# A hybrid encoder step on one core: ScalarE makes the third factor of the queries' norms behind its copy of the values and the keys' squares instead of ahead of them

## What is computed

```python
def mla_queries(cq_raw, pos, q_a_norm, w_q_up, q_nope_norm, q_rope_norm):
    B, T, _ = cq_raw.shape
    q = (rmsnorm(cq_raw, q_a_norm) @ w_q_up).reshape(B, T, MLA_HEADS, QK_NOPE + QK_ROPE)
    q_nope = rmsnorm(q[..., :QK_NOPE], q_nope_norm)
    q_pe = rope(rmsnorm(q[..., QK_NOPE:], q_rope_norm), pos)
    return q_nope, q_pe

def mla_expand(ckv, w_kv_up, k_nope_norm):
    B, S, _ = ckv.shape
    kv = (ckv @ w_kv_up).reshape(B, S, MLA_HEADS, QK_NOPE + V_HEAD)
    return rmsnorm(kv[..., :QK_NOPE], k_nope_norm), kv[..., QK_NOPE:]
```

## Time and profile before

| | before |
|---|---|
| median of 3 runs | 1995.39 us (1994.79 to 1996.48) |
| the profiled execution | 1995.78 us |
| its span, first to last instruction | 1994.0 us |
| PE busy | 1985.5 us (100%) |
| DVE busy | 1254.3 us (63%) |
| ACT busy | 911.5 us (46%) |
| POOL busy | 192.7 us (10%) |
| granted TensorE clock, mean | 0.999 |

### The profile page before, as it was taken

The page is one execution under the profiler, slowest core; times in us unless marked ns, Lnnn a source line. Parts: engine busy times, 40 slices in busy tenths (PEclk is TensorE's granted clock), DMA queues, the critical chain, the costliest instruction groups (busy, mean ns, idle before and its releaser), DMA issues.

```text
span 1994.0 us, 36219 instructions
## 1 busy us (share of the span) xinstructions
PE 1985.5 (100%) x14762; PEld 1961.7 (98%) x14762; DVE 1254.3 (63%) x2474; ACT 911.5 (46%) x1810; POOL 192.7 (10%) x228
## 2 busy tenths in 40 slices
PE   9999999999999999999999999999999999999998
PEld 9999999999999999999999999999999999999998
DVE  7856677677576786868777555444455664444444
ACT  5564456565444443434444444444444553333333
POOL 0011143433200000000000001000000000000000
PEclk9999999999999999999999999999999999999999
DMA  9765443333455554645545655565556556666665
GB/s 249 197 187 157 113 120 117 99 111 119 122 170 147 149 169 128 179 127 175 157 145 170 169 169 168 168 170 168 173 169 171 169 183 193 193 193 193 193 193 142
DMA packets 219262, 323.24 MB, mean 162 GB/s; under 512 B 28240, under 2 KB 100264, under 8 KB 219096
## 3 DMA queue, kind: packets, MB, share of 16 engines
q1 hardware_dynamic: 215800, 317.71, 55.3%
q10 hardware_dynamic: 3296, 3.22, 0.5%
HBM read 310.06 MB, written 9.62 MB: 160 GB/s over the span
## 4 chain that ended last, share of the span: by engine, by line
PE 99%; DVE 0%; DMA 0%; ACTq 0%; ACT 0%; issue 0%
PE bank L1884 31%; PE bank L1887 30%; PE bank L1888 30%; PE bank L2150 1%; PE bank L2120 1%; PE bank L2046 1%; PE bank L2049 1%; PE bank L2048 1%; PE bank L2222 0%; PE bank L2248 0%; PE bank L2116 0%; PE bank L2117 0%; DMA xt<-in_meta_tokens_dram 0%; PE bank L2260 0%; PE bank L2064 0%; PE bank L2065 0%
## 5 line engine op out<-in xcount | busy, mean ns | idle before, releaser
L1215 DVE TENSOR_TENSOR wlo<-raw,whi 128x512 fp32r<-128x512 f32 (+1 forms) x1256 | 811.0, 655 | 681.5 <-ACT whi L801 671.5
L1884 PE MATMUL bank<-xsplit,whi 128*128 128x288 f32 (+2 forms) x4128 | 1217.2, 295 | 2.4 <-DVE xsplit L1239 2.1
L1888 PE MATMUL bank<-xsplit,wlo 128*128 128x288 f32 (+2 forms) x4128 | 1212.1, 294 | 0.0
L1887 PE MATMUL bank<-xsplit,whi 128*128 128x288 f32 (+2 forms) x4128 | 1211.9, 294 | 0.0
L801 ACT CAST whi<-raw 128x512 fp32r<-128x512 f32 (+1 forms) x1256 | 706.8, 576 | 954.9 <-PE bank L1888 911.6
L1884 PEld LDWEIGHTS bank<-xsplit,whi 128*128 128x128 f32 (+1 forms) x4128 | 773.2, 187 | 5.1 <-issue 3.4
L1887 PEld LDWEIGHTS bank<-xsplit,whi 128*128 128x128 f32 (+1 forms) x4128 | 773.2, 187 | 2.0 <-issue 1.0
L1888 PEld LDWEIGHTS bank<-xsplit,wlo 128*128 128x128 f32 (+1 forms) x4128 | 772.8, 187 | 0.0
L1884 PE MATMUL bank<-latents,whi 128*128 128x288 f32 (+1 forms) x352 | 112.7, 320 | 0.2
L1887 PE MATMUL bank<-latents,whi 128*128 128x288 f32 (+1 forms) x352 | 106.9, 304 | 0.0
L1888 PE MATMUL bank<-latents,wlo 128*128 128x288 f32 (+1 forms) x352 | 106.7, 303 | 0.0
(11 more groups left out here) (301 smaller groups left out, 1254.8 us busy)
## 6 DMA issues: line engine op xcount, KB each, us to landing
raw<-in_w_in_dram SPq DMA_DIRECT2D x313, 512.0 KB, 3.8
raw<-in_w_out_dram SPq DMA_DIRECT2D x128, 512.0 KB, 3.8
raw<-in_w_in_dram SPq DMA_DIRECT2D x142, 256.0 KB, 3.1
raw<-in_w_q_up_dram SPq DMA_DIRECT2D x48, 384.0 KB, 3.3
raw<-in_w_kv_up_dram SPq DMA_DIRECT2D x16, 512.0 KB, 3.7
xres<-in_x_prompt_dram SPq DMA_DIRECT2D x32, 128.0 KB, 3.7
xt<-in_x_prompt_dram SPq DMA_DIRECT2D x28, 128.0 KB, 4.9
out_dram<-ytok SPq DMA_DIRECT2D x28, 128.0 KB, 3.5
```

The source lines that it names most:

```text
L1215: ins = tt(lo, src, hi.bitcast(f32), ALU.subtract)
L1884: ins = mm(out, w_hi, m_hi, start=start, stop=False, **kw)
L1887: mm(out, w_hi, m_lo, start=False, stop=False, **kw)
L1888: return mm(out, w_lo, m_hi, start=False, stop=stop, **kw)
```

## The change

`q_rstd` takes a list of the factors to make. Behind unit 15 (unit 14 in the first pair) it now makes the first two; the third is made at the end of `pair_end`, behind the copy of the values and the two squares of the keys.

```diff
-            def q_rstd(phase, i, n):
+            def q_rstd(phase, i, n, tiles):
 
-                for t in range(3):
+                for t in tiles:
                     b = 4 + t
...
                 k_square_hi(phase, i, n, 0)
                 k_square_hi(phase, i, n, 1)
+                q_rstd(phase, i, n, (2,))
...
                 if k == 14:
-                    q_rstd("bulk0", 0, 0)
+                    q_rstd("bulk0", 0, 0, (0, 1))
...
                     if k == 15 and phase == "step":
-                        q_rstd(phase, i, j + 1)
+                        q_rstd(phase, i, j + 1, (0, 1))
```

## The result

The changed kernel takes 2000.82 us, median of 10 runs (1999.94 to 2001.42), beside 1995.47 us for the kernel before in runs on the same chip: 1.0025 times as long, 95% interval 1.0017 to 1.0033. It is slower by some 5 us, where 4.7 were forecast. Its profiled execution has a span of 1999.0 us, 5.0 more than before.

A forecast was written before the change was run, and what follows sets the result against it. TensorE bounds, meeting the ACT-DVE-POOL chain without slack. 6 x 0.79 x 0.96 = 4.55 plus 0.3 for the first pair, 4.85, taken as 4.7, gave 2000.5 profiled, 2000.1 us predicted; range 1996.4 to 2001.6.

The forecast's parts named there:

- PE and the chain meet with no slack: At the transposes PE waits for POOL's probabilities, so 0.96 of a delay in the chain reaches the pair's end.
- The copy of the values is not held by the factor: At a pair's end the copy waits for PE's last matmul, starting 0.04 us behind it.
- a little faster: Rival: the copy of the values starts sooner and PE's 0.16 us stall shrinks; at most 1.1 us, 1994.3; chance 0.03.
- Casts 0.87 later, unit 3 0.32 later, turn 1.9 later: Delays in us at a pair's end: ACT's casts, unit 3 reaching DVE, and POOL's turn of the queries.
- Lost turns: DVE held by POOL running beside it: 0.28 us by the turn, 0.88 by four copies, against 0.69 before.
- Both close encounters: POOL's second copy against DVE's unit 4 first part, DVE not held; third copy against first scaling, POOL first.
- one turn fewer: Rival: DVE's first scaling precedes POOL's third copy, so a turn of 0.22 to 0.26 us falls away; 1998.7; chance 0.20.
- The rule of the Trainium skill: Shared SBUF ports go to whichever of DVE and POOL starts first; taken literally, chain about 0.87 us later, 2000.7.
- Scalings end 0.79 later: DVE's scaling of queries, and the chain behind it, moves 0.32 + 0.28 + 0.88 - 0.69 us in six pairs.
- Not slower: POOL out of DVE's way: Rival: today's three lost DVE turns (0.69 us) vanish and cover the casts' delay; 1995.4; chance 0.17.
- The sum: Six pairs give 4.55 us, the first 0.3: 4.85, taken as 4.7 since pair 398's late exponentials may cover some.
- The last pair: At 500 us the next group's maxima wait 1.12 us for PE, not this chain, so cost 0.

The follow-up runs named there:

- short copies in the kernel before: Kernel before with POOL's four copies of turned queries 72 instead of 288 columns wide, the rest left out: 1995.13 us, ratio 0.9998.
- the last experiment: Changed kernel, Ln and Exp moved behind units 3 and 4's casts, and PE's third tile of unit 0 behind unit 1's first two: 1994.01 us, ratio 0.9992.
- late casts alone: Kernel before with four idle ACT copies ahead of the casts of units 3 to 5 in seven pairs: 1995.87 us, ratio 1.0001.
- a late turn alone: Kernel before with POOL's turn of the queries waiting for ACT's cast of unit 4 of the next pair: 1996.07 us, ratio 1.0003.
- both put in by hand: Kernel before with four idle ACT copies ahead of the casts and POOL's turn waiting for the last of them: 2000.69 us, ratio 1.0026.

## Why the prediction was right

Predicted 2000.1 us, measured 2000.8, and by the path that was forecast.

- *Bounds: PE and the chain meet with no slack.* Shown from both sides: 0.73 earlier gains nothing (short copies in the kernel before), 0.37 later at the exponentials costs 0.35 a pair.
- *The copy of the values is not held by the factor.* It starts 0.04 behind PE's last matmul in both kernels, now with 0.94 idle ahead. The rival "a little faster" fell with it. That its price was well estimated shows in the last experiment: the stall of 0.16 a pair is real, but to win it the tile has to move, not the factor.
- *Casts 0.87 later, unit 3 0.32 later, turn 1.9 later.* Measured 0.87, 0.32 (2.89 against 2.57) and 1.91 (2.54 against 0.63). (The working's "0.09 before an end" is 0.11 by the row that it names; from the Exp's start to the casts it took 0.35, where 0.36 was taken.)
- *Lost turns.* 0.28 + 0.88 = 1.16 were forecast against 0.69 before; 1.17 and 0.68 were found. That the first total is so near is in part luck: the turn held unit 3's first part for 0.33 and not 0.28, since it started 0.05 later, and the four copies cost 0.84 and not 0.88. Both close encounters came out as forecast: DVE's unit 4 at 336.00 took 0.41 though POOL's copy had started at 335.98, and the first scaling at 336.77 was held by the copy at 336.76. So "one turn fewer" fell. At the first encounter POOL's copy took 0.71, where the copies before and behind it took 0.50 and 0.42, as if POOL was the one held. The rule of the Trainium skill ("SBUF — State Buffer", section "SBUF: two separate sides"), that whoever starts first has the ports, is not borne out by the rows at the first of these, where the one that starts second by the profile was not held; its 2000.7 is near the measured time by the sizes below, not by this turn.
- *Scalings end 0.79 later.* Measured 0.81. "Not slower: POOL out of DVE's way" fell: side by side work of 3 us was what happened. Moving the factor further still is the way in which POOL does get out of DVE's way.
- *The sum.* The part of a delay that reaches the pair's end, 0.96 from a single pair's 0.27 of 0.28, held: the five middle pairs other than that at 398 grew by 0.75 to 0.79 for a scaling's end 0.81 later. Three terms were mis-sized, all a little low. The scalings' end was put at 0.79. In the pair at 398 the late exponentials were given up to 0.28 to cover the cost, for which 4.85 became 4.7; they covered nothing (34.77 against 33.93, 0.84 more), since that lateness of ACT came on top again. (The prediction's 2000.7 leaves this cover out; with it, it would be 2000.5.) The first pair was put at 0.3 and took 0.39. So 6 pairs of 0.75 to 0.84 and 0.39 make 5.1 instead of 4.7. In the profiled spans that is 5.0. The medians differ by 5.35, since the profiled execution of the kernel before lies 0.31 above the median of its runs here (1995.78 against 1995.47) and that of the changed kernel at its own; the interval of the ratio (3.4 to 6.6 us) is wider than that.
- *The last pair.* Put at 0 and found at 0.

## What to carry to other kernels

Where an engine off the bound gets a wait moved, don't ask only who waits for it, but beside whom it will then run: here POOL, which waits, had time to spare, and the price was paid by DVE beside it. Two delays that are each hidden can cost in full together, since one takes the slack that hides the other; so a move is costed with all its consequences in one timeline, and not consequence by consequence. And a small move of an instruction that is not urgent may be best made larger: two units further on the same Ln and Exp cost nothing.

## What the runs showed that was not expected

ACT's exponentials in the pair near 398 are 0.28 late in the earlier trace rows, with DVE's maxima on time. In the changed kernel the same instruction is late by the same (413.37 above, 2.02 idle instead of 1.72), and so it is in five of the experiments. In the three where idle copies were added to ACT ahead of it, it is not, as in the one with late casts alone:

```profile
409.70 0.38 ACT L996 ACTIVATE prob<-bank,nmax 128x144 f32<-128x144 f32 x1 [1.72 <-DVE nmax L1466]
```

DVE shows the like at one place near 297, in the second of the keys' rests, hidden in the changed kernel by the wait for the casts:

```profile
299.50 0.61 DVE L1417 TENSOR_TENSOR sqr<-sqb,ksh 128x432 fp32r<-128x432 f32 x1 [0.19 <-issue]
```

POOL shows it in two experiments, in the pair that starts near 467 or 469: its turn of the queries starts 0.29 later than in the other pairs with a late turn alone (2.96 instead of 2.67) and with both put in by hand (2.80 instead of 2.51). The first of these pairs is 33.66 long, since the units pass ahead of the turn, and the second 34.74.

So the lateness goes with a place in an engine's order and not with a wait in the program; it cost the kernel before 0.27 us of span. The traces show one thing more that goes with these places. The page lists two DMA queues of instructions. This is the smaller one, with 50 packets of 8 KB (packets, MB and share of 16 engines):

```profile
q14 instruction: 50, 0.41, 0.1%
```

In the seven kernels in which the exponentials are late they are the 704th instruction recorded on ACT, and such a packet starts 0.95 to 1.46 us behind them. With idle copies ahead of them they are the 715th or 724th, and the packet starts when 702 to 706 instructions of ACT have started, beside casts that are on time. DVE's late rest is the 448th on DVE in all ten kernels, and a packet starts 0.66 to 0.94 behind it; behind POOL's late turn one starts 0.63 or 0.68 later. That the loading of instructions makes the lateness, and why it shows at some of these places and not at others, no run here shows, and it stays open.
